# Expert weights loaded in pairs of tiles with 16 KB rows, and the setup's small tables issued from ScalarE's queue

## The reference

```
def modulation(cvec, p):
    return jnp.split(jax.nn.silu(cvec) @ p['mod_w'] + p['mod_b'], 6, axis=-1)

h2 = rmsnorm(x, p['norm2_pre']) * (1.0 + m_lat[4]) + m_lat[3]
x = x + m_lat[5] * rmsnorm(expert_choice_moe(h2, p), p['norm2_post'])

def expert_choice_moe(h, p):
    affinity = jax.nn.softmax((h @ p['router_w']).astype(jnp.float32), axis=-1)
    gates, idx = lax.top_k(jnp.swapaxes(affinity, 1, 2), cap)
    xe = jax.vmap(lambda hb, ib: hb[ib])(h, idx)
    hid = jax.nn.silu(jnp.einsum('becd,edf->becf', xe, p['exp_w1'])) * jnp.einsum('becd,edf->becf', xe, p['exp_w3'])
    ye = jnp.einsum('becf,efd->becd', hid, p['exp_w2']) * gates[..., None].astype(h.dtype)
    ...
```

## Time and profile before

| | |
|---|---|
| median of 3 executions | 2384.78 us |
| profiled execution | 2384.09 us |
| span of its profile | 2382.2 us |
| mean granted clock of PE | 0.855 |
| PE busy | 1848.8 us (78%) |
| DVE busy | 844.1 us (35%) |
| ACT busy | 644.1 us (27%) |
| POOL busy | 266.2 us (11%) |
| HBM read | 584.95 MB |

### The profile page before, as it was taken

How to read it: one execution, slowest core, us unless ns; L and a number is a source line. 1 busy time by engine, 2 the same in 40 slices (tenths; PEclk the granted TensorE clock), 3 DMA queues, 4 the chain that set the end, 5 groups by cost and what they waited for, 6 DMA issues and landing times. The chain is left out here.

```text
span 2382.2 us, 36573 instructions
## 1 busy us (share of the span) xinstructions
PE 1848.8 (78%) x15419; PEld 1219.7 (51%) x15419; DVE 844.1 (35%) x1230; ACT 644.1 (27%) x1035; POOL 266.2 (11%) x329
## 2 busy tenths in 40 slices
PE   6998988978999877798888967666666666666665
PEld 6997977867778766697777853111111111111110
DVE  4654345765555565577564551000000000000001
ACT  4434445554324344333442430000000000000001
POOL 0100013420211043201450000000000000000000
PEclk9999998999999887898997988777777777876777
DMA  6654642337996410061002458999999999999997
GB/s 201 197 179 152 187 148 71 103 126 246 287 293 218 136 36 2 13 189 58 3 3 76 160 207 355 423 423 424 423 424 423 423 423 424 423 423 423 424 423 305
DMA packets 197408, 588.14 MB, mean 247 GB/s; under 512 B 10671, under 2 KB 143822, under 8 KB 156318
## 3 DMA queue, kind: packets, MB, share of 16 engines
q1 hardware_dynamic: 196200, 585.57, 64.3%
q10 hardware_dynamic: 1078, 0.70, 0.1%
HBM read 584.95 MB, written 1.28 MB: 246 GB/s over the span
## 5 line engine op out<-in xcount | busy, mean ns | idle before, releaser
L3327 PE MATMUL ps<-ex_ring,ex_xe 128*32 128x512 f32 x1536 | 279.3, 824 | 148.4 <-DMA ex_ring<-in_exp_w 148.3
L3404 DVE TENSOR_TENSOR ex_hid<-ps,ex_silu 128x512 f32<-128x512 f32 x16 | 11.1, 692 | 879.9 <-PE ps L3327 879.9
L3327 PEld LDWEIGHTS ps<-ex_ring,ex_xe 128*32 128x32 f32 x1536 | 37.2, 125 | 383.5 <-DMA ex_ring<-in_exp_w 360.2
L209 PE MATMUL ps<-xt_hi,ffn_whi 128*128 128x256 f32 x704 | 205.5, 292 | 7.3 <-DVE xt_lo L372 7.3
L3350 PE MATMUL ps<-ex_ring,ex_ht 128*32 128x512 f32 x768 | 132.7, 825 | 95.6 <-DMA ex_ring<-in_exp_w 95.6
L210 PE MATMUL ps<-xt_lo,ffn_whi 128*128 128x256 f32 x704 | 201.2, 286 | 0.0
L211 PE MATMUL ps<-xt_hi,ffn_wlo 128*128 128x256 f32 x704 | 201.1, 286 | 0.0
L181 DVE TENSOR_TENSOR ffn_wlo<-ring,ffn_whi 128x2048 fp32r<-128x2048 f32 x66 | 154.3, 2338 | 109.3 <-ACT ffn_whi L174 108.9
L174 ACT CAST ffn_whi<-ring 128x2048 fp32r<-128x2048 f32 x66 | 125.1, 1900 | 109.2 <-PE ps L211 94.9
L209 PEld LDWEIGHTS ps<-xt_hi,ffn_whi 128*128 128x128 f32 x704 | 137.2, 195 | 17.5 <-issue 16.5
L210 PEld LDWEIGHTS ps<-xt_lo,ffn_whi 128*128 128x128 f32 x704 | 137.0, 195 | 1.3 <-issue 1.3
(11 more groups left out here) (760 smaller groups left out, 4103.6 us busy)
## 6 DMA issues: line engine op xcount, KB each, us to landing
ex_ring<-in_exp_w SPq DMA_DIRECT2D x192, 1024.0 KB, 27.4
ex_ring<-in_exp_w SPq DMA_DIRECT2D x48, 2048.0 KB, 33.3
ring<-in_exp_w SPq DMA_DIRECT2D x64, 1024.0 KB, 27.2
ring<-in_w_in SPq DMA_DIRECT2D x55, 1024.0 KB, 5.2
ring<-in_exp_w SPq DMA_DIRECT2D x16, 2048.0 KB, 29.1
ring<-in_ffn_w_gate SPq DMA_DIRECT2D x22, 1024.0 KB, 6.3
ring<-in_ffn_w_up SPq DMA_DIRECT2D x22, 1024.0 KB, 5.4
ring<-in_ffn_w_down SPq DMA_DIRECT2D x22, 1024.0 KB, 4.9
```

The source lines that it names most:

```text
L209: nc.tensor.matmul(out, lhs[0], rhs[0], start=start, stop=False, skip_group_check=shared)
L3327: mm = mm_(ps[32 * q:32 * q + 32, 4 + u, :], xe[:, k], expert_slot(g, n)[:, 512 * q:512 * q + 512], start=k == 0, stop=k == KC - 1)
L3404: v.tensor_tensor(hid[:], ps[:, 5, :], silu[:], ALU.mult).then_inc(S["hid"], 1)
```

## The change

Features are laid out two apart. A chunk of 256 features is now split by even and odd instead of into halves: `paired` views a row of features as (chunk j, column c, h), so that partition p of the tiles 2j and 2j + 1 holds the features 256 j + 2 p and 256 j + 2 p + 1. Those two rows of w1 or w3 are neighbours in DRAM, and one load of 2 MB brings 16 KB in one piece for each partition. All expert tiles are loaded two at a time, into two neighbouring slots, when both are free, and PE waits once in two tiles.

The order of the features has to be the same in the tokens. So the router reads the normed tokens (its turning matmuls and its gathering ones) with a step of two elements, loads its table in the paired order, and takes shift and scale in that order. These come from the modulation: the two sums that the router needs are loaded a second time as 8 rows of 256 values, turned with 8 more small matmuls, and three operations of DVE make shift and scale from them in place of two. For the biases and the norm in this order the setup loads 12 more rows of 256 values (`wide`), turns them with two more transposes and copies them with one more copy to `pairs`. In the setup, the four small tables (rel_bias, onehot, mask, lambda vectors) are issued from ACT's queue, behind its rows and the two new loads, in place of SP's.

```diff
@@ setup_phase
-        n_rows = 16 * (len(VEC_A) + len(VEC_B) + 1 + 6)
+        n_rows = 16 * (len(VEC_A) + len(VEC_B) + 1 + 6 + 2)
...
+            act.dma_start(wide[0:8], I["mod_b_2"][0:1, 3 * D:5 * D].rearrange("l (r n) -> (l r) n", n=T)).then_inc(S["rows"], 16)
+            act.dma_start(wide[8:12], I["norm2_pre_2"].rearrange("l (r n) -> (l r) n", n=T)).then_inc(S["rows"], 16)
+            act.dma_start(buckets[:, 0:BIAS_HEADS], I["rel_bias"]).then_inc(S["buckets"], 16)
+            act.dma_start(buckets[:, BIAS_HEADS:], I["k_onehot"]).then_inc(S["buckets"], 16)
+            act.dma_start(dmask[:], I["k_dmask"]).then_inc(S["buckets"], 16)
+            act.dma_start(lamv[:, 0:256], I["diff_lambda"].rearrange("l a b -> l (a b)").to_broadcast([P, 256])
+                          ).then_inc(S["lam"], 16)
...
             load_tiles(g, sp, 2)
-            sp.dma_start(buckets[:, 0:BIAS_HEADS], I["rel_bias"]).then_inc(S["buckets"], 16)
-            sp.dma_start(buckets[:, BIAS_HEADS:], I["k_onehot"]).then_inc(S["buckets"], 16)
-            sp.dma_start(dmask[:], I["k_dmask"]).then_inc(S["buckets"], 16)
-            sp.dma_start(lamv[:, 0:256], I["diff_lambda"].rearrange("l a b -> l (a b)").to_broadcast([P, 256])
-                         ).then_inc(S["lam"], 16)
             load_tiles(g, sp, R)
...
+            for h in range(2):
+                nc.tensor.transpose(g.ps[:, 3, 12 * h:12 * h + 12], paired(wide[:])[:, 0, h], g.ident[0:12, 0:12])
...
+            nc.vector.tensor_copy(g.pairs[:].rearrange("p h r -> p (h r)"), g.ps[:, 3, 0:24])
@@ Modulation
+        sp.dma_start(self.pair_sums, self.sums_dram[:, 0, 3 * D:5 * D].rearrange("j (m q) -> m j q", q=256)).then_inc(S["mod_back"], 16)
...
-            pe.wait_ge(self.S["mod_back"], 32)
+            pe.wait_ge(self.S["mod_back"], 48)
+            for h in range(2):
+                for j in range(4):
+                    self.nc.tensor.matmul(self.ps[:, 0, 96 + 8 * h:104 + 8 * h], paired(self.pair_sums[:, j])[:, 0, h],
+                                          self.g.ident[0:8, 0:8], start=j == 0, stop=j == 3)
...
+        ch.add(v.tensor_tensor(router_shift, shift2, mod_b3, ALU.add))
+        ch(v.tensor_tensor(router_scale, scale2, mod_b4, ALU.add))
+        ch(v.scalar_tensor_tensor(router_scale, router_scale, 1.0, norm2, ALU.add, ALU.mult))
@@ merge_phase
-            for i in range(out0, out0 + R):
-                sp.wait_ge(g.tiles_split, i + 1)
-                load_expert_tile(nc, g, sp, I, 0, i % R, i % R)
+            freed = {s: max(i for i in range(out0, out0 + R) if i % R in (s, s + 1)) for s in (0, 2)}
+            for s in sorted(freed, key=freed.get):
+                sp.wait_ge(g.tiles_split, freed[s] + 1)
+                load_expert_pair(nc, g, sp, I, 0, s, s)
@@ load_expert_pair
+def paired(x):
+    return x.rearrange("p (j c h) -> p j h c", h=2, c=P)
+
+def load_expert_pair(nc, g, sp, I, e, j, n):
     if j < 2 * KC:
+        src = I[("exp_w1_2", "exp_w3_2")[j // KC]][0].rearrange("e (k p h) f -> p (e k) (h f)", h=2, p=P)
     else:
+        src = I["exp_w2_2"][0].rearrange("e (k p h) n -> p (e k) (h n)", h=4, p=P)
+    s = n % ER
+    dst = (g.ring[:, s:s + 2, :] if s < R else g.ex_ring[:, s - R:s - R + 2, :]).rearrange("p s n -> p (s n)").unsqueeze(1)
+    sp.dma_start(dst, src[:, bass.ds(4 * e + j % KC // 2, 1), :]).then_inc(g.ex_loaded[s], 16)
@@ router_phase
-            sp.dma_start(rw[:], I["router_w_2"][0].rearrange("(k p) e -> p k e", p=P)).then_inc(S["consts"], 16)
+            sp.dma_start(rw[:].rearrange("p (j h) e -> p j (h e)", h=2), I["router_w_2"][0].rearrange("(j p h) e -> p j (h e)", p=P, h=2)
+                         ).then_inc(S["consts"], 16)
...
-            for j in range(R, ER):
-                load_expert_tile(nc, g, sp, I, 0, j, j)
+            for j in range(R, ER, 2):
+                load_expert_pair(nc, g, sp, I, 0, j, j)
...
-                    mm = nc.tensor.transpose(ps[:, k // 2, T * (k % 2) + P * t:T * (k % 2) + P * t + P], g.xn[:, t, P * k:P * k + P], g.ident[:])
+                    mm = nc.tensor.transpose(ps[:, k // 2, T * (k % 2) + P * t:T * (k % 2) + P * t + P],
+                                             paired(g.xn[:, t])[:, k // 2, k % 2], g.ident[:])
...
-                        mm = nc.tensor.matmul(ps[:, k % 4, :], x[:, t, P * k:P * k + P], pick[:, t].rearrange("p e s -> p (e s)"),
+                        mm = nc.tensor.matmul(ps[:, k % 4, :], paired(x[:, t])[:, k // 2, k % 2], pick[:, t].rearrange("p e s -> p (e s)"),
@@ expert_phase
-            for n in filter(begins_load, range(ER, turn)):
-                sp.wait_ge(used, n - ER + (1 if n % TPE < 2 * KC else 2))
-                load_expert_tile(nc, g, sp, I, n // TPE, n % TPE, n)
+            for n in range(ER, turn, 2):
+                sp.wait_ge(used, n - ER + 2)
+                load_expert_pair(nc, g, sp, I, n // TPE, n % TPE, n)
...
-                        pe.wait_ge(g.ex_loaded[n % ER], loaded(ee, n))
+                        if n % 2 == 0:
+                            pe.wait_ge(g.ex_loaded[n % ER], loaded(ee, n))
```

More of the change, by code:

```diff
@@ L1566, in allocate @@
     g.ident, g.va, g.vb = sb("ident", [P, P]), sb("va", [P, NA]), sb("vb", [P, NB])
-    g.ones = sb("ones", [P, T])
+    g.ones, g.pairs = sb("ones", [P, T]), sb("pairs", [P, 2, 12])
     g.lam, g.ss = sb("lam", [P, 1]), sb("ss", [P, 8])
@@ L1952, in dve_end @@
         m3 = g.mod[:].rearrange("p (m r) -> p m r", r=2)
+        shift2, scale2 = (self.ps[:, 0, 96:112].rearrange("p (h m j) -> p m j h", h=2, m=2)[:, m] for m in range(2))
+        mod_b3, mod_b4, norm2 = (g.pairs[:].rearrange("p h (m j) -> p m j h", m=3)[:, m] for m in range(3))
+        router_shift, router_scale = (x[:, 2, :].rearrange("p (j h) -> p j h", h=2) for x in (g.shift, g.scale))
+        ch.add(v.tensor_tensor(router_shift, shift2, mod_b3, ALU.add))
+        ch(v.tensor_tensor(router_scale, scale2, mod_b4, ALU.add))
+        ch(v.scalar_tensor_tensor(router_scale, router_scale, 1.0, norm2, ALU.add, ALU.mult))
         v.tensor_tensor(m3, self.ps[:, 0, 0:96].rearrange("p (r m) -> p m r", r=2),
@@ L1957, in dve_end @@
             v.tensor_tensor(self.post[:, j], m3[:, KC * m:KC * m + KC, 0], col(g, name, 0, KC), ALU.mult).then_inc(S["post"], 1)
-        for j, (m, r, norm) in enumerate(((1, 0, "norm1_pre_2"), (1, 1, "norm1_pre_2"), (4, 0, "norm2_pre_2"))):
+        for j, (m, r, norm) in enumerate(((1, 0, "norm1_pre_2"), (1, 1, "norm1_pre_2"))):
             ch.add(v.scalar_tensor_tensor(g.scale[:, j, :], m3[:, KC * m:KC * m + KC, r], 1.0, col(g, norm, 0, KC), ALU.add, ALU.mult))
-        for j, (m, r) in enumerate(((0, 0), (0, 1), (3, 0))):
+        for j, (m, r) in enumerate(((0, 0), (0, 1))):
             ch.add(v.tensor_copy(g.shift[:, j, :], m3[:, KC * m:KC * m + KC, r]))
@@ L3135, in expert_slot @@
     return g.ring[:, i, :] if i < R else g.ex_ring[:, i - R, :]
-def begins_load(n):
-    return n % TPE < 2 * KC or n % 2 == 0
-def load_expert_tile(nc, g, sp, I, e, j, n):
-    slot = expert_slot(g, n)
+def paired(x):
+    return x.rearrange("p (j c h) -> p j h c", h=2, c=P)
+def load_expert_pair(nc, g, sp, I, e, j, n):
     if j < 2 * KC:
-        w = I[("exp_w1_2", "exp_w3_2")[j // KC]][0].rearrange("e (k p) f -> p (e k) f", p=P)
-        src = w[:, bass.ds(KC * e + j % KC, 1), :]
-        dst = slot.unsqueeze(1)
-    else:
-        src = I["exp_w2_2"][0].rearrange("e (k p h) n -> p (e k) (h n)", h=4, p=P)[:, bass.ds(4 * e + j % KC // 2, 1), :]
-        s = n % ER
-        dst = (g.ring[:, s:s + 2, :] if s < R else g.ex_ring[:, s - R:s - R + 2, :]).rearrange("p s n -> p (s n)").unsqueeze(1)
-    sp.dma_start(dst, src).then_inc(g.ex_loaded[n % ER], 16)
+        src = I[("exp_w1_2", "exp_w3_2")[j // KC]][0].rearrange("e (k p h) f -> p (e k) (h f)", h=2, p=P)
+    else:
+        src = I["exp_w2_2"][0].rearrange("e (k p h) n -> p (e k) (h n)", h=4, p=P)
+    s = n % ER
+    dst = (g.ring[:, s:s + 2, :] if s < R else g.ex_ring[:, s - R:s - R + 2, :]).rearrange("p s n -> p (s n)").unsqueeze(1)
+    sp.dma_start(dst, src[:, bass.ds(4 * e + j % KC // 2, 1), :]).then_inc(g.ex_loaded[s], 16)
 def router_phase(nc, g, I, xet, mt, aff):
@@ L3292, in loaded @@
         def loaded(ee, n):
-            mine = [m for m in range(n % ER, turn, ER) if begins_load(m)]
-            return ee * (16 * len(mine)) + 16 * len([m for m in mine if m <= n])
+            return ee * (16 * turn // ER) + 16 * (n // ER + 1)
         @block.sync
@@ L3299, in _ @@
             sp.dma_start(post[:], g.post_dram[0:1, 1].to_broadcast([P, D])).then_inc(S["post"], 16)
-            for n in filter(begins_load, range(ER, turn)):
-                sp.wait_ge(used, n - ER + (1 if n % TPE < 2 * KC else 2))
-                load_expert_tile(nc, g, sp, I, n // TPE, n % TPE, n)
+            for n in range(ER, turn, 2):
+                sp.wait_ge(used, n - ER + 2)
+                load_expert_pair(nc, g, sp, I, n // TPE, n % TPE, n)
```

(6 more changed lines are left out.)

4 lines of the change are left out of this document (3 added, 1 removed).

## The result

The changed kernel takes 2368.39 us in the median of 6 runs (2367.32 to 2375.65), the kernel before, beside it, 2383.03 (2378.13 to 2394.31): ratio 0.9935, 95% interval 0.9906 to 0.9964. A ratio is taken over all executions and is not that of the two medians, which stand beside it. The profiled execution took 2369.01 us (before 2384.09), and its span is 2367.2 us.

A forecast was written before the change was run, and what follows sets the result against it. Compute was taken to bound the kernel up to about 1450 us, the expert-weight stream after. Terms -9.1 - 2.2 + 1.6 = -9.7 us gave 2374.4 on the profiled execution, 2375.1 against the median; range 2369 to 2383.

The forecast's parts named there:

- What bounds the kernel: Whole kernel: compute sets the pace up to about 1450 us, the stream of expert weights from then on.
- The rival of PE as the bound: Experts: PE, waiting for whole pairs, gets less clock and becomes the slower bound; +16 us, 2401; chance 0.04.
- the one in which row length brings little: Experts: row length is not what makes w2 faster; about -2.5 us in all, 2382.3; chance 0.13.
- Pairs, -9.1: Expert weights: 120 pairs of w1 and w3 tiles land in 4.906 instead of 4.982 us; -9.1 us, bounds 5.4 to 12.6.
- the rival: All terms at their best: stream gains 12.6, setup 3.6, modulation costs 0.8; -15.4 us, 2369.4; chance 0.27.
- Coarser waits, 0: Ring of expert weights: freeing and loading two slots at once, and PE waiting for a pair, cost 0.
- Setup, -2.2: Setup: small tables on ScalarE's queue end it at 17.95 instead of 20.17 us; -2.2 us, bounds nothing to -3.6.
- Modulation, +1.6: Modulation, where PE is full: 16 added matmul instructions at 0.101 us each; +1.6 us, bounds 0.8 to 2.1.
- Router, 0: Router: strided weights for 16 transposes and 32 gathering matmuls cost 0; bounds 0 and +1.5 us.
- The rule on the packet's overhead: Expert weights: about 3 fixed cycles a packet would make pairs gain only 0.029 us each, 3.5 us in all.
- The rule on several queues: Setup: issuing DMAs from several engines saves only issue time, so the tables' gain would be about 1.1 us.

The follow-up runs named there:

- e4: The kernel before with w2 too in 1 MB loads of 8 KB rows, so no 16 KB rows are left; ratio 1.0021.
- g1: The kernel before, unchanged, profiled once more; 2396.46 us.
- e2: The kernel before with only the four small tables moved to ScalarE's queue; ratio 0.9982, 2381.48 us.
- e3: The kernel before with w1 and w3 in 2 MB loads, two tiles at a time, but still 8 KB rows; ratio 0.9992.
- g2: The changed kernel, unchanged, profiled and timed again; ratio 0.9955, 2374.23 us.
- g3: The changed kernel, unchanged, timed once more beside two other kernels; ratio 0.9956, 2375.2 us.
- e5: The changed kernel without its 8 small modulation matmuls, router shift and scale taken from other sums; 2366.21 us in its one execution.
- e6: The changed kernel with the modulation's partial sums brought as 32 rows and added in 2 matmuls instead of 8; ratio 0.9929, 2366.64 us.
- g6: The kernel of e6 again, unchanged, with more rounds; ratio 0.9941, 2370.21 us.
- e8: The changed kernel with features four apart everywhere, w1 and w3 in 4 MB loads of 32 KB rows, sums added in 4 matmuls; ratio 0.9938, 2369.43 us.
- e7: The changed kernel with w1 and w3 in 4 MB loads of 32 KB rows, tokens not put in matching order; ratio 0.993.

## Why the forecast was right or wrong

- **What bounds the kernel.** Right. The stretch from the experts' first matmul to the last landing follows the rate of the stream in every run: 921.8 (e4), 917.3 (before, g1, e2), 916.6 (e3), 906.1 to 906.7 (changed, g2, g3, e5, e6, g6), 901.9 and 902.2 (e8, e7). PE starts each pair on its landing; its clock moved between 0.73 and 0.81 without effect. The rival of PE as the bound is out, and so is the one in which row length brings little, by e3 and e4.
- **Pairs, -9.1.** Measured -10.7. The mechanism held, the size of a pair was off: 4.906 came from w2 in a mixed stream, and in a stream of one form it is 4.893. 0.013 by 120 is the missing 1.6 us. It lies inside the bounds given (5.4 to 12.6), and the rival named this cause ("the stream of one form only runs at the better bound"), though not as far as its 12.6.
- **Coarser waits, 0.** Right: e3 has all of them and not the rows, and loses nothing.
- **Setup, -2.2.** Measured -2.0, in the changed kernel and alone in e2, with causal's issue the next thing late, as the step said.
- **Modulation, +1.6.** Measured +3.4, outside its bounds of 0.8 to 2.1. The row's own busy time, 0.129, was taken as the upper bound and was nearly the price (0.124), so the instructions cost 2.0 instead of 1.6; the step had no term for the clock behind them, 1.6 us.
- **Router, 0.** Right: 193 ns two apart against 188, over 32 loads some 0.2 us. The nearest row that the step used was four apart and at a lower clock, and there the step is free (231 ns against 230); at the higher clock four apart it is not (311 ns, e8). The upper bound of 1.5 should have been 1.8 by its own working (16 by 0.115).
- **The sum.** -10.7 - 2.0 + 3.4 - 0.4 (the tail) = -9.7, the forecast's -9.7. Two mis-sized terms, +1.8 and -1.6, nearly cancel, which is luck. By the repeats' ratios the gain is 10.7 and 10.5 us.
- **What failed is the range: it had no term for the scatter of executions.** The prediction said that three executions of the kernel before differ by 13 us and used it for a tenth of a chance; the range's low end, 2369, took only the terms at their best, from one base. The base itself moved: 2384.78 in three executions was 2383.03 in the six beside the changed kernel, 1.75 of the 6.7 us between the forecast of 2375.1 and 2368.39, and from that base the low end would have been 2367.3. A stretch ahead of the experts in which the clock is 0.5 or 1.0 by execution is 11.5 us by itself (g1), and medians of 6 runs still carry some of it: the three ratios of the same kernel are 0.9935, 0.9955 and 0.9956. With some 4 us of that on either side the low end would have been 2365. By the repeats, the first measured 0.65% is about 0.44% of change and 0.2% of that scatter.
- **The rule on the packet's overhead.** 8 KB against 16 KB rows differ by 0.089 us per 2 MB. The Trainium skill ("DMA: Bandwidth & Descriptors", Why small descriptors are slow) gives a few cycles a packet, which I had worked out to an estimate of 0.029 us a pair and 3.5 us in all; measured is 10.7, three times as much, and the rows of w2 were the better guide.
- **The rule on several queues.** Moving four tables from SP to ScalarE gave 2.0 us. The Trainium skill ("DMA: Bandwidth & Descriptors", Issuing engines are not separate DMA queues) would have it save only the issues' own time, which I had put at 1.1 us. Here the gain is of another kind: with the tables moved, SP stands 3.0 to 4.5 us in single issues of weights and causal (2.98 to 4.46 in e2), ScalarE meanwhile issues each small table in 0.4 to 0.5, and PE, which needs them, starts 3.43 us earlier.

## What to carry to other kernels

Where a stream of loads fills the DMA engines, lengthen the contiguous row of a partition; the size of the load and the number of waits did nothing, and the gain shrinks with each doubling. Keep small tables off the queue that issues the big loads. Where PE is full, a matmul of a few rows costs as much as one of 96 rows (0.124 and 0.114 us an instruction here), and twice that with its weights four elements apart (0.24): put partial sums on more rows and add them in one matmul instead of accumulating over several. And before 10 us are forecast or judged on a kernel with stages of small matmuls, compare two executions of the same kernel stage by stage.
